# Gate and up projections of a two-layer hybrid decoder as seven block products in place of eight

## The reference

```python
for l in range(DEPTH):
    m, c_new, sg_new, sr_new = _mixer(_rmsnorm(h, norm_mix_pre[l]), pos, ...)
    h = h + _rmsnorm(m, norm_mix_post[l])
    f = _swiglu(_rmsnorm(h, norm_ffn_pre[l]), w_gate_up[l], w_down[l])
    h = h + _rmsnorm(f, norm_ffn_post[l])

def _swiglu(hn, w_gate_up, w_down):
    gu = hn @ w_gate_up                    # 1024 x 5632
    gate, up = jnp.split(gu, 2, axis=-1)
    return (jax.nn.silu(gate) * up) @ w_down
```

## Time and profile before

| what | value |
|---|---|
| median of 3 runs | 1434.93 us (1433.58 to 1436.19) |
| profiled execution, span from first to last instruction | 1431.1 us |
| TensorE busy | 1413.0 us (99%) |
| VectorE busy | 850.7 us (59%) |
| ScalarE busy | 544.2 us (38%) |
| mean granted TensorE clock | 0.996 |

### The profile page before, as it was taken

The page is one execution under the profiler, slowest core; times in us unless marked ns, Lnnn a source line. Parts: engine busy times, 40 slices in busy tenths (PEclk is TensorE's granted clock), DMA queues, the critical chain, the costliest instruction groups (busy, mean ns, idle before and its releaser), DMA issues.

```text
span 1431.1 us, 29170 instructions
## 1 busy us (share of the span) xinstructions
PE 1413.0 (99%) x12580; PEld 1390.9 (97%) x12580; DVE 850.7 (59%) x1393; ACT 544.2 (38%) x1050; POOL 99.7 (7%) x141
## 2 busy tenths in 40 slices
PE   9999999999999999999999999999999999999997
PEld 8999999999999999999989999999999999999996
DVE  7745895877555554332486569868775555543224
ACT  5135463556222222322342364643652222232222
POOL 0001211100000000000000012111000100000000
PEclk9999999999999999999999999999999999999998
DMA  5332332122343343222213313412323333322221
GB/s 202 108 103 71 97 114 81 60 89 81 111 142 137 139 136 119 89 89 94 84 60 112 110 60 97 120 60 74 96 74 121 137 140 137 137 97 89 92 100 61
DMA packets 57695, 147.45 MB, mean 103 GB/s; under 512 B 19040, under 2 KB 22496, under 8 KB 57568
## 3 DMA queue, kind: packets, MB, share of 16 engines
q1 hardware_dynamic: 49744, 119.89, 24.9%
q0 software_dynamic: 7824, 25.70, 5.0%
HBM read 132.79 MB, written 12.78 MB: 102 GB/s over the span
## 4 chain that ended last, share of the span: by engine, by line
PE 92%; DVE 5%; ACT 1%; issue 1%; DMA 0%; SPq 0%; DVEq 0%; ACTq 0%
PE PS L577 77%; PE PS L583 5%; DVE hT L1664 1%; DVE Wl L1626 1%; DVE Xl L1643 1%; DVE mT L1663 1%; PE PS L771 1%; PE PS L1100 1%; PE PS L755 0%; PE PS L917 0%; PE PS L743 0%; PE PS L753 0%; PE PS L822 0%; PE PS L596 0%; PE PS L1021 0%
## 5 line engine op out<-in xcount | busy, mean ns | idle before, releaser
L577 PE MATMUL PS<-Xh,Wh 128*128 128x260 f32 x2464 | 504.2, 286 | 2.6 <-DVE Xl L1685 2.2
L577 PE MATMUL PS<-Xl,Wh 128*128 128x260 f32 x2464 | 497.8, 283 | 0.0
L577 PE MATMUL PS<-Xh,Wl 128*128 128x260 f32 x2464 | 495.9, 283 | 0.0
L1168 ACT ACTIVATE Wh<-stage 128x1024 fp32r<-128x1024 f32 x211 | 223.6, 1060 | 661.9 <-PE PS L577 643.7
L577 PEld LDWEIGHTS PS<-Xh,Wh 128*128 128x128 f32 x2464 | 382.3, 189 | 7.6 <-DVE Xl L1685 2.6
L577 PEld LDWEIGHTS PS<-Xh,Wl 128*128 128x128 f32 x2464 | 379.9, 188 | 0.0
L577 PEld LDWEIGHTS PS<-Xl,Wh 128*128 128x128 f32 x2464 | 379.6, 189 | 0.0
L1626 DVE TENSOR_TENSOR Wl<-stage,Wh 128x1024 fp32r<-128x1024 f32 x211 | 257.9, 1222 | 181.8 <-ACT Wh L1168 181.3
L577 PE MATMUL PS<-actH,Wh 128*128 128x260 f32 x616 | 124.1, 283 | 0.0
L577 PE MATMUL PS<-actH,Wl 128*128 128x260 f32 x616 | 124.0, 282 | 0.0
L577 PE MATMUL PS<-actL,Wh 128*128 128x260 f32 x616 | 123.7, 282 | 0.0
(11 more groups left out here) (327 smaller groups left out, 1600.5 us busy)
## 6 DMA issues: line engine op xcount, KB each, us to landing
stage<-w_slabs SPq DMA_DIRECT2D x211, 512.0 KB, 3.3
dst<-state_ret POOLq DMA_DIRECT2D x32, 256.0 KB, 3.2
dst<-state_gdn POOLq DMA_DIRECT2D x32, 256.0 KB, 3.1
out_gdn_sample<-dst POOLq DMA_DIRECT2D x16, 256.0 KB, 2.8
out_ret_sample<-dst POOLq DMA_DIRECT2D x16, 256.0 KB, 3.1
hT<-x_t SPq DMA_DIRECT2D x3, 520.0 KB, 7.0
out_y_t<-hT SPq DMA_DIRECT2D x3, 520.0 KB, 3.0
hT<-x_t SPq DMA_DIRECT2D x2, 260.0 KB, 3.6
```

Source lines behind the costliest of these rows:

```text
L577: ins = mm(pj(slot)[:, a], w[:, ws, pos, :], x[:, a, :], start=first and w is Wh and x is xh, stop=last and w is Wl)
L1168: A(Wh[:, G % NW], stage[:, G % NS], ACT.Copy).then_inc(s["hi_split"], 1)
```

## The change

17 of the 22 pairs of each layer (`Q = 17`; the first 5, `NP`, stay as they were) are no longer computed as two tiles of 8 blocks. A pair is seen as a 2 by 2 block matrix: rows are gate and up, columns the two halves of the 1024 input features; the activations are 2 by 2 as well, feature halves by column halves. The usual product of these needs 8 block products; the change uses a scheme with 7, each of 4 blocks of 128 by 128 with 260 columns, three matmuls per block. The seven products are issued in the order `UA11, US2, US1, UA12, US3, US4, UA22`, called products 1 to 7 below. The price is sums: of weight halves before (`w_sum2`, `w_sum4` on VectorE), of activations once per layer (`x_scaled`, `x_sum`, `x_low`, and ScalarE's `weighted`, `x_high`), and of results after (`post`: `U2, TD, C22, C12, C21`). Products 5, 6 and 7 add onto a PSUM bank that `U2`, `TD` and `C22` must have read first.

The weights of such a pair come as quarters of 256 KB: `UA11` in one transfer (its semaphore is `b11_loaded`), then three transfers with the semaphore `b2_loaded`: the first quarter of the up tile to two places at once (512 KB written), and two further quarters (256 KB each). The two buffer sets `A` and `B` alternate; a third, `C`, serves pair 0 only. From pair 3 on SyncE issues the `b2` transfers of pair q+1 when product 6 of pair q-1 is done. Set `A` takes the place of `Xh` and `Xl`, set `B` that of the staging, `Wh` and `Wl` buffers.

The activations of all 22 pairs are split into `actH` and `actL` only during and after the last pair, since these buffers lie where the summed activations are. The 16 outer products, their operands, the state updates and GpSimd's transfers that follow them move to the down stage, one per slab. Some semaphores are merged into shared counters, and some buffers get another place.

```diff
+    NP = 5
+    Q = FT - NP
+    UN = 7
...
+    UA11, US2, US1, UA12, US3, US4, UA22 = range(UN)
+    POSTS = 5
...
+            def quarters(l, q):
+                N = l * Q + q
...
+                elif q < 3:
+                    sp.wait_ge(s["tile_done"], l * TILES + T_DN)
+                else:
+                    sp.wait_ge(s["p_done"], (N - 2) * UN + US1 + 1)
+                if N:
+                    sp.wait_ge(s["b11_loaded"], N * 16)
+                sp.dma_start(w[:, UA11], quarter(l, q, 0, 0)).then_inc(s["b11_loaded"], 16)
+                if q >= 3:
+                    sp.wait_ge(s["p_done"], (N - 2) * UN + US4 + 1)
...
+                sp.dma_start(w[:, US1:US3 + 1:2], quarter(l, q, 1, 0).unsqueeze(1).to_broadcast([P, 2, QW])).then_inc(s["b2_loaded"], 16)
+                sp.dma_start(w[:, US4], quarter(l, q, 1, 1)).then_inc(s["b2_loaded"], 16)
+                sp.dma_start(w[:, UA12], quarter(l, q, 0, 1)).then_inc(s["b2_loaded"], 16)
...
+                    for u, bank in enumerate((a_, b_, c_, a_, b_, c_, b_)):
+                        if q == 0:
+                            pe.wait_ge(s["ffn_rest"], l * REST + 8 + u + 1)
+                        if u % 2 == 0:
+                            pe.wait_ge(s["ffn_rest"], l * REST + X_STEPS + q * W_STEPS + W_LO + u // 2)
...
+                        elif u == US3:
+                            pe.wait_ge(s["post_done"], N * POSTS + U2)
+                        elif u == US4:
+                            pe.wait_ge(s["post_done"], N * POSTS + TD)
+                        elif u == UA22:
+                            pe.wait_ge(s["post_done"], N * POSTS + C22)
+                        for k in range(4):
+                            cols = slice(k * P, (k + 1) * P)
+                            mm(PS[:, bank, 0:HC], hi_[:, u, cols], XU[:, u, 0, k], start=k == 0 and u < 3, stop=False, skip_group_check=True)
+                            mm(PS[:, bank, 0:HC], hi_[:, u, cols], XU[:, u, 1, k], start=False, stop=False, skip_group_check=True)
+                            ins = mm(PS[:, bank, 0:HC], lo_[:, u, cols], XU[:, u, 0, k], start=False, stop=k == 3, skip_group_check=True)
...
-                for i in range(3, 2 * FT):
+                for i in range(3, 2 * NP):
...
+                for q in range(Q):
+                    strassen(q)
...
+                        if b == 7:
+                            rows_back()
+                        elif b % 8 == 7 and 2 <= b // 8 < 18:
+                            outer(b // 8 - 2)
...
+                def weighted(k):
...
+                    A(to, hT[:, k], ACT.Copy, scale=prm[:, l, row:row + 1]).then_inc(s["ffn_round"], 1)
...
+                def w_high(q, c):
...
+                    A(hi_[:, us], full[:, us], ACT.Copy).then_inc(s["ffn_round"], 1)
...
+                for j in range(NP):
...
+                    if j == 0:
+                        for k in range(KT):
+                            weighted(k)
                     act.wait_ge(s["tile_free0"], (T0 + T_GU + 2 * j) // 2 + 1)
-                    A(gp[:], gp[:], ACT.Silu).then_inc(s["gate_silu"], 1)
...
+                for q in range(Q):
+                    if q:
+                        gate_second(q - 1)
+                    first_copy(q)
+                    if q + 1 < Q:
+                        w_high(q + 1, 0)
+                        w_high(q + 1, 1)
+                        gate_first(q)
+                        w_high(q + 1, 2)
+                        w_high(q + 1, 3)
+                    else:
+                        act_high(0, 2)
...
+                def w_sum2(q):
...
+                    V.tensor_tensor(w[:, US1:US3 + 1:2], w[:, US1:US3 + 1:2], w[:, UA11:US4 + 1:US4], ALU.add).then_inc(s["ffn_rest"], 1)
...
+                    V.tensor_tensor(w[:, US2], w[:, US1], w[:, US4], ALU.add).then_inc(s["ffn_rest"], 1)
...
+                def w_sum4(q):
...
+                    V.tensor_tensor(w[:, UA22], w[:, US2], w[:, UA12], ALU.add).then_inc(s["ffn_rest"], 1)
...
+                def w_low(q, c):
...
+                    V.tensor_tensor(lo_[:, us], full[:, us], plain(hi_[:, us]), ALU.subtract).then_inc(s["ffn_rest"], 1)
...
+                def post(q, n):
...
+                    if n == U2:
+                        ins = V.tensor_tensor(u2, PS[:, b_, 0:HC], p1, ALU.add)
+                    elif n == TD:
+                        ins = V.tensor_tensor(tdif[:], PS[:, c_, 0:HC], p1, ALU.subtract)
+                    elif n == C22:
+                        ins = V.tensor_tensor(up[:, 1], tdif[:], PS[:, b_, 0:HC], ALU.subtract)
+                    elif n == C12:
+                        ins = V.tensor_tensor(up[:, 0], PS[:, c_, 0:HC], u2, ALU.subtract)
+                    else:
+                        ins = V.tensor_tensor(gp[:, 1], PS[:, b_, 0:HC], p1, ALU.add)
...
+                    if j == 0:
+                        x_scaled(0)
...
+                    else:
+                        w_sum2(0)
+                        w_sum4(0)
                     done(t + 1)
-                    freed(V.tensor_tensor(up[:], pj(1), rb[:], ALU.mult), t + 1)
+                    freed(V.tensor_tensor(up, pj(1), rb[:], ALU.mult), t + 1)
...
+                        for c in range(3):
+                            w_low(0, c)
...
+                for q in range(Q):
+                    last = q == Q - 1
+                    if q:
+                        post(q - 1, C21)
+                    w_low(q, 3)
+                    if q:
+                        gated(q - 1)
+                    if not last:
+                        w_sum2(q + 1)
+                    else:
+                        rest_act(0, 2)
+                    post(q, U2)
+                    if not last:
+                        w_sum4(q + 1)
+                    else:
+                        rest_act(2, 2)
+                    post(q, TD)
+                    if not last:
+                        w_low(q + 1, 0)
+                        w_low(q + 1, 1)
+                    else:
+                        lo(G0 + S_DN)
+                        rest_act(4, 2)
+                    post(q, C22)
+                    if not last:
+                        w_low(q + 1, 2)
+                    else:
+                        rest_act(6, 2)
+                    post(q, C12)
...
```

More of the change, by code:

```diff
@@ L250, in trunk, with w_set, acc_banks, plain @@
         B_V = (6, 4, 5, 6)
-        vblks = [vblk0[:], vblk[:]]
+        vblks = [vblk[:, 0], vblk[:, 1]]
+        gp, up = (sqb[:, i].rearrange("p (a n) -> p a n", a=2) for i in range(2))
+        def w_set(q):
+            return (loC, hiC, fullC) if q == 0 else (loB, hiB, fullB) if q % 2 else (loA, hiA, fullA)
+        def acc_banks(q):
+            return (0, 1, 2) if q % 2 else (4, 5, 6)
+        def plain(ap):
+            return ap.bitcast(fp32)
+        def x_full(u):
+            return XF[:, u, 1]
+        def act_full(j):
+            return actF[:, j] if j < FT - 2 else (act20, act21)[j - FT + 2][:]
+        def act_low(j):
+            return actL[:, j] if j < FT - 2 else actL2[:, j - FT + 2]
+        def quarter(l, q, up_, k):
+            return w_slabs[l, S_GU + 2 * (NP + q) + up_, :, k * QW:(k + 1) * QW]
         QR = 32
@@ L2168, in _ @@
+                lo(G0 + S_DN + 1)
+                rest_act(8, 2)
+                post(Q - 1, C21)
+                rest_act(10, 2)
+                gated(Q - 1)
+                rest_act(12, 2)
+                lo(G0 + S_DN + 2)
+                for j in range(14, FT - 2, 2):
+                    rest_act(j, 2)
+                rest_act(FT - 2, 1)
+                rest_act(FT - 1, 1)
                 step(V.memset(ss[:], 0.0))
@@ L2178, in _ @@
                             down_tile(k)
+                    if 2 <= i < 18:
+                        new_state(i - 2)
                 down_tile(KT - 2)
```

354 lines of the change are left out of this document (270 added, 84 removed).

## The result

| what | before | changed |
|---|---|---|
| median time, 4 runs each | 1434.26 us (1433.11 to 1436.19) | 1465.76 us (1460.70 to 1468.83) |
| ratio, 95% interval | | 1.0226 [1.021, 1.0243] |
| profiled execution, span | 1431.1 us | 1464.0 us |
| mean granted TensorE clock | 0.996 | 0.986 |

The forecast was 1422 us, faster, with a range up to 1447. The kernel became 31.5 us slower. The 49.0 us of matmuls did go; some 82 us of losses came (49.0 and the 32.9 between the spans).

The account below looks back on a forecast made before the run. TensorE was taken as the bound, busy 99% of the span. Per layer 24.5 - 5.0 - 3.3 - 1.9 - 7.7 = 6.6 us, 13.2 for two layers, gave a median of 1421.7 us, range 1409 to 1447.

Parts of the forecast that it names:

- What is removed: Block products on TensorE: 84 matmuls per pair in place of 96, saving 24.5 us per layer, 49.0 in all, the ceiling.
- Entry: Entry of gate and up stage: fourth tile 4.5 us late behind new VectorE and ScalarE work, another 0.5 later; 5.0 per layer.
- Start: Start of block products: TensorE waits 2.8 us for product 1's first low part, plus 0.5 in pair 0, per layer.
- Later pairs: Every pair after pair 0: 0.5 us idle each from late b2 loads, 15 pairs, 7.7 us per layer.
- D: Time from end of product 6 of pair q-1, when b2 transfers start, to their landing: 4.85 us, range 4.6 to 5.46.
- s = (D - 3.82)/2: Mean TensorE idle time per later pair, met ahead of product 7 in two pairs; 0.52 us at D = 4.85.
- Clock: Granted clock falls after the entry and start stops: 1.0 + 0.9 = 1.9 us of work lost per layer.
- Rival 3: Short idle time in every pair brings the clock down, 1.5 us less 0.5 swallowed, 32 times: 1454 us; chance 6%.
- Down stage and no cost elsewhere: Down stage as long as before but for 16 outer products of 0.24; VectorE's lists and activation sums cost nothing.
- Rival 2: Loads slower: D = 6.6, pairs lose 20.9 us per layer, 1448 us; break-even at D = 5.7; chance 22%.
- Rival 4: Products pack less closely because each begins with several waits: 0.1 us each, 24 us in all, 1446 us; chance 7%.
- Rival 1: Waits shorter: clock holds through both stops and D is 4.6; 10.3 us gained per layer, 1414 us; chance 20%.

Follow-up runs that it names:

- experiment 12: Changed kernel with early loads, entry work moved, C22 behind one low part, doubled quarter loaded once, first low part early, pair 0 evacuations reordered: 1388.33 us, ratio 0.9697.
- experiment 3: Changed kernel with the doubled up quarter loaded once (256 KB in place of 512 KB), VectorE making both sums from it: 1428.17 us, ratio 0.9975.
- experiment 9: Changed kernel with early loads, entry work moved, and C22 behind one low part of the next pair's weights in place of two: 1399.79 us, ratio 0.977.
- experiment 4: Changed kernel with the b2 transfers from pair 3 on started after product 7 in place of product 6: 1516.52 us, ratio 1.0586.

## Why the prediction was wrong, step by step

**What is removed: right.** Matmuls with `XU` start 0.12 us apart, 408 fewer. The ceiling of 49 us is real: experiment 12 reaches 43.8 of it.

**Entry: right.** Forecast 4.5 and 0.5 us plus 1.0 for the clock. Measured: 4.08 later at the fourth tile, clock 0.57 from 347.0 to 350.5 (1.5 us of work), together 5.6 against 6.0. The stop of 0.5 did not come and the clock cost 0.5 more, so that the sum fits in part by luck. Taking it away gave 12.8 us for two layers, 11.0 if each is measured against the kernel before on its own chip.

**Start: the stop right, the clock too small.** TensorE stopped for 2.71 us, forecast 2.8. The clock behind it was low for longer than the 3.0 us of the earlier trace rows:

```profile
391.50:396.00 4.50, 4.34 (x20) 4.37 (x21) 3.66 (x5) 0.39 (x1) 0.00 (x0) 0.50 0.70 250
396.00:398.00 2.00, 2.00 (x12) 2.00 (x12) 1.95 (x4) 0.69 (x1) 0.00 (x0) 0.55 0.72 189
```

That is 2.2 + 0.9 = 3.1 us of work lost, where 0.9 was forecast. I had also let a 0.5 us wait of pair 0 swallow part of it, and that wait did not come: at half speed the product needed its input later.

**Later pairs: the step that failed, twice.** Forecast: 0.5 us each, 7.7 per layer. (It counted 15 pairs with such loads; there are 14 in a layer.) Measured: the 17 pairs of the first layer took 204.1 us (391.7 to 595.8) for 171.4 of work; less the 3.1 of clock at the start, 29.6 us lost.

First the size of D, "the time from there to their landing". I took 4.85 from a slab and two stores and held 5.46 for the upper end. It is 6.03, and over 6.8 in a quarter of the pairs. The rate was not far off: 266 GB/s from 475.20 to 477.50 and 262 to 479.00, against the 293 of the earlier trace rows, but next to nothing moves in the first 1.2 us after the first issue (25 GB/s from 473.96 to 475.20), and three issues are 0.94 apart. I had seen the row for a landing of 256 KB behind another (4.6 us) and used it as an end, not as what it said: that the last of several transfers lands late. Bounds from other sizes and directions were no bounds. The long landings, those with an `instruction` packet 3.9 to 4.7 us after the issue, are a term that the prediction put at nothing.

The Trainium skill, "DMA: Bandwidth & Descriptors", section Bandwidth, has 6.15 us of transfer for 1 MB, measured with GpSimd as the issuer, not SyncE. The trace has 6.0 from issue to first sum, waiting for the issues and the first data included, so the figure is above what was moved here (some 4.8 us of transfer). As a warning it was better than my rows: by it the layer would have lost 17.5 us in the pairs and come out 3.2 us slower than before.

Then the formula, s = (D - 3.82)/2. It "met twice" the idle time ahead of product 7 and took product 5 as never late. That holds for a D under 5.14 only, as experiment 3 shows (10.6 us a pair at 4.56, the formula 10.45). The chain of the profile is another: `U2` stands behind the two sums on VectorE, and product 5 needs it. Above 5.14 the pair takes D + 5.6, so that s = D - 4.5, with slope 1. It is borne out from 5.73 to 7.83: 5.97 gives 11.57 (measured 11.57), 7.35 gives 12.95 (12.96), the other pairs of full clock agree within 0.02, and 6.01 with the issue 2.18 later gives 13.8 (13.7 to 13.8). With my formula a D of 6.03 costs 1.1 us, with the right one 1.5. I had worked out the list of VectorE up to `C22` and not asked of the evacuations on the way who waits for each.

So the 29.6 are 14 pairs at 1.5 us for a D of 6.0 (21.3), 4.6 for what D was beyond 6.0, nearly all of it in the pairs with an `instruction` packet behind the issue, and 2.8 for two falls of the clock; 0.9 is left for the other pairs. The falls too came with the late loads: the three in the pairs stand behind the three longest D (7.35, 7.37, 7.83). The load with 7.35 made a pair of 12.96 us (product 5 at 444.90 and at 457.86), and the clock that fell behind its stop of 1.90 us made the next one 12.94, though its own D was 6.06. A median D does not carry that.

**Clock: neither safe nor lost each time.** Rival 3 gave 32 falls. There were three in the 34 pairs, behind stops of 1.89, 1.90 and 2.34 us; those of up to 1.85 us left it at 1.00. The Trainium skill, "TensorE: Matmul & The Clock Gate", section on HAM oscillation, tells of a kernel cold at each tile behind transfers of 3 to 5 us; here the stops were shorter, and the trace shows full clock behind most of them. The mean clock of 0.986 is 15 us of the time all the same, 9 of them at the two entries and starts.

**Down stage and no cost elsewhere: right.** 115.0 us in place of 111.0, all by the outer products moved there; ahead of it only product 7 of the last pair waited, 0.34 us.

**Rival 2** named the place: VectorE waits for `b2` ahead of L2387. It gave 0.22 for a time of 1448 at D = 6.6 and put the break-even at 5.7. The measured D lies between, and the time beyond both, since the rival used the same formula. Of the forecast's own chance too much stood on one value of D whose upper end was 0.24 from break-even. **Rival 4** fell: no gaps between products in 152 us. **Rival 1** fell.

## What to carry to other kernels

When a transfer is issued inside a loop by the work that frees its buffer, write the loop down as a circle (free, issue, land, each instruction queued behind the wait, the product that needs it) and look for the shortest way round, not only the last: here the nearer consumer had slope 1. Issue each piece when its own buffer is free; this cost nothing and moved the kernel from 2.3% slower to 0.9% faster. And gains of separate edits add only where they don't meet in the same loop: early loads and the new order of VectorE's list gained 46 and 18 us alone, and together no more than the order did, while the order of experiment 9 went with the early loads. Last, look at the spread of a landing time and at the profile's `instruction` queue, not at a median alone.

## What the runs showed of the hardware

A landing time is not a size over a rate. 256 KB issued alone landed in 2.7 us; 1 MB in three transfers behind one another had its first reader at 6.0 us, and 768 KB at 4.65 (medians).

The same three transfers took 6.85 to 7.83 us in seven of 28 pairs, and each of these had a packet of 16 KB on the queue `instruction` that started 3.9 to 4.7 us after the first issue; the 21 others had none there and took 5.73 to 6.35. With 768 KB the pairs with such a packet took 5.09 to 6.14, those without 4.26 to 4.81. In experiment 4 no such packet fell between issue and first sum, and no landing took over 6.20. There are 96 of them in the changed kernel (1.57 MB), a cost that no line of the kernel shows.

The clock behind a stop is not told by its length. In the changed kernel it fell behind 1.89, 1.90 and 2.34 us and stayed behind 1.85. In the pairs of experiment 4, 25 stops were of 2.64 to 2.89 us; sixteen left it at 1.00 and nine came with a fall, while three of 1.98 to 2.27 us left it at 1.00. The fall can come later than the stop, too: behind the 1.90 us before 457.86 the matmuls ran at 0.12 us until 459.26, then at 0.215 until about 462.5. Here are these two stretches:

```profile
457.90:459.30 1.40, 1.40 (x12) 1.40 (x13) 1.40 (x3) 1.40 (x2) 0.00 (x0) 0.97 0.00 0
459.30:462.50 3.20, 3.20 (x16) 3.20 (x16) 3.20 (x5) 1.90 (x4) 0.00 (x0) 0.50 0.00 0
```

What decides it stays open.
